# Attention in a fused block: how the softmax's inverse sums reach the output

## The reference, cut to what matters

```python
h = rms_norm(x, attn_norm_g[i])
q, k, v, u, vv = jnp.split(h @ w_in[i], split_at, axis=-1)
q, k = rms_norm and axial_rope of q and k, per head
# gqa_attention, per block of queries:
sc = jnp.einsum('bqkgd,bskd->bkgqs', qblk, k).astype(jnp.float32) * scale
p = jax.nn.softmax(sc, axis=-1).astype(v.dtype)
attn_o = jnp.einsum('bkgqs,bskd->bqkgd', p, v)
sg_o = spatial_gating(gelu(u), gelu(vv), sg_norm_g[i], sg_w[i], sg_b[i])
merged = concat([rms_norm(attn_o, attn_out_g[i]), rms_norm(sg_o, sg_out_g[i])])
x = x + merged @ w_o[i]
# then a gated FFN with a depthwise convolution
```

## Time and profile before

| | |
|---|---|
| median of 3 runs | 2430.03 us (2429.65 to 2431.97) |
| the profiled execution, its own time | 2432.05 us |
| its span in the profile | 2430.2 us |
| TensorE busy | 2377.9 us, 98% of the span |
| VectorE, ScalarE, GpSimd busy | 60%, 44%, 8% |
| chain that ended last | TensorE 84%, VectorE 11%, ScalarE 2% |

### The profile page before, as it was taken

The page is one execution under the profiler, slowest core; times in us unless marked ns, Lnnn a source line. Parts: engine busy times, 40 slices in busy tenths (PEclk is TensorE's granted clock), DMA queues, the critical chain, the costliest instruction groups (busy, mean ns, idle before and its releaser), DMA issues.

```text
span 2430.2 us, 33037 instructions
## 1 busy us (share of the span) xinstructions
PE 2377.9 (98%) x11655; PEld 1939.3 (80%) x11655; DVE 1469.2 (60%) x2142; ACT 1078.0 (44%) x1456; POOL 202.8 (8%) x239
## 2 busy tenths in 40 slices
PE   8999999999999999999999999999999999999999
PEld 6766888888778878888888777888888867888887
DVE  7986654532677646554226867887533686687722
ACT  5345533332555645333225644554423573454421
POOL 2010100000100011000005111000011322000000
PEclk9999999999999999999999999999999999999999
DMA  7331233333222222333334103333334302233331
GB/s 176 70 96 49 82 99 92 101 90 101 71 82 74 78 70 87 95 96 94 94 105 114 56 10 87 104 104 95 93 98 119 101 10 70 87 104 95 91 95 65
DMA packets 403511, 212.30 MB, mean 87 GB/s; under 512 B 19411, under 2 KB 398935, under 8 KB 403431
## 3 DMA queue, kind: packets, MB, share of 16 engines
q1 hardware_dynamic: 397111, 199.65, 28.6%
q0 software_dynamic: 5984, 11.53, 2.0%
q10 hardware_dynamic: 336, 0.05, 0.0%
HBM read 204.38 MB, written 4.19 MB: 86 GB/s over the span
## 4 chain that ended last, share of the span: by engine, by line
PE 84%; DVE 11%; ACT 2%; issue 1%; DVEq 1%; DMA 0%; ACTq 0%; SPq 0%
PE bank L687 69%; PE bank L733 4%; DVE tmp L1958 2%; PE bank L737 2%; DVE w_lo L1926 2%; PE bank L1316 1%; DVEq L1955 1%; DVE small L2711 1%; PE bank L763 1%; PE bank L1290 1%; PE bank L1258 1%; PE bank L1182 0%; PE bank L1128 0%; DVE tmp L1967 0%; PE bank L1219 0%
## 5 line engine op out<-in xcount | busy, mean ns | idle before, releaser
L1926 DVE TENSOR_TENSOR w_lo<-w_raw,w_hi 128x1024 fp32r<-128x1024 f32 x380 | 472.3, 1243 | 522.8 <-ACT w_hi L1390 518.2
L687 PE MATMUL bank<-h_hi,w_hi 128*128 128x512 f32 x1840 | 726.5, 395 | 2.2 <-DVEq L1955 1.2
L687 PE MATMUL bank<-h_lo,w_hi 128*128 128x512 f32 x1840 | 717.9, 390 | 0.0
L687 PE MATMUL bank<-h_hi,w_lo 128*128 128x512 f32 x1840 | 717.6, 390 | 0.0
L1390 ACT ACTIVATE w_hi<-w_raw 128x1024 fp32r<-128x1024 f32 x380 | 401.7, 1058 | 628.1 <-PE bank L687 610.7
L687 PEld LDWEIGHTS bank<-h_hi,w_hi 128*128 128x128 f32 x1840 | 346.6, 188 | 77.5 <-issue 3.8
L687 PEld LDWEIGHTS bank<-h_lo,w_hi 128*128 128x128 f32 x1840 | 346.2, 188 | 72.5
L687 PEld LDWEIGHTS bank<-h_hi,w_lo 128*128 128x128 f32 x1840 | 346.5, 188 | 72.1 <-issue 1.9
L687 PE MATMUL bank<-hid_hi,w_hi 128*128 128x512 f32 x704 | 273.9, 389 | 0.0
L687 PE MATMUL bank<-hid_hi,w_lo 128*128 128x512 f32 x704 | 273.9, 389 | 0.0
L687 PE MATMUL bank<-hid_lo,w_hi 128*128 128x512 f32 x704 | 273.9, 389 | 0.0
(11 more groups left out here) (469 smaller groups left out, 2873.6 us busy)
## 6 DMA issues: line engine op xcount, KB each, us to landing
w_raw<-in_ffn_w SPq DMA_DIRECT2D x120, 512.0 KB, 3.8
w_raw<-in_w_up SPq DMA_DIRECT2D x88, 512.0 KB, 3.8
w_raw<-in_c_w_in SPq DMA_DIRECT2D x32, 512.0 KB, 4.0
w_raw<-in_w_down SPq DMA_DIRECT2D x32, 512.0 KB, 3.6
w_raw<-in_w_in SPq DMA_DIRECT2D x28, 512.0 KB, 3.9
w_raw<-in_w_o SPq DMA_DIRECT2D x16, 512.0 KB, 3.6
w_raw<-in_ab_w_in SPq DMA_DIRECT2D x12, 512.0 KB, 6.1
w_raw<-in_ffn_w SPq DMA_DIRECT2D x16, 384.0 KB, 3.2
```

Source lines behind the costliest of these rows:

```text
L687: mm = nc.tensor.matmul(out[:], w[:, s, k], v[:, kt], start=(kt == 0 and w is w_hi and v is hi), stop=(kt == sum(slabs) - 1 and v is lo))
L1926: nc.vector.tensor_tensor(w_lo[:, s], w_raw[:, s], w_hi[:, s].bitcast(F32), ALU.subtract).then_inc(lo_done, 1)
```

## The change: what it does

Each unit gets its own inverse sum. VectorE takes the reciprocal of one column of `total` per unit (`shares(u)`), GpSimd makes of it a diagonal 128 by 128 (`share_diagonal`: the identity times that column), and T(u) is now four `matmul` calls of `prob` with this diagonal instead of four `transpose` calls with the identity; it waits for `diag_made`. So what is turned is already divided by its sum. The spreads, `keep_share` and `head_out` go. Values are done as whole query tiles: eight products in every second unit from u = 6, instead of four in each. The step from the row maximum to the shift moves from VectorE to GpSimd (`negated_top`, behind a new semaphore `top_ready`). The head outputs are read from the value bank: ScalarE takes the high part and now also the square (`oa_sq`), VectorE the low part, GpSimd only adds the squares. GpSimd's steps are now an order written out by hand as well: in turn u the diagonal of u+1, the shift of u+3, and at u = 5, 7, 9, 11 the squares and sums of a gate tile, at u = 13, 21, 29 the addition for a head pair.

The diff, without the list of semaphore names and unchanged lines:

```diff
@@ -29,7 +29,7 @@
...
 MIX_AT = (4, 6, 8, 10)
-SHARE_AT = (12, 20, 28)
+HEAD_AT = (12, 20, 28)
 SCORE_BANKS = ((2, 3, 4), (0, 1, 4))
@@ -316,11 +316,11 @@
...
         ua_lo = m("ua_lo", [P, 4, SEQ], 8, F32R)
-        oa = m("oa", [P, SEQ], 16)
+        oa_sq = m("oa_sq", [P, SEQ], 16)
+        diag = s5_v[:].rearrange("p v g -> p (v g)").rearrange("p (b q) -> p b q", b=4)
         ua_sum = sq_sum
...
         part_sq = m("part_sq", [P, SEQ], 54)
-        share_all = mixed
         inv_ua = m("inv_ua", [P, SEQ], 48)
...
@@ -582,23 +582,45 @@
...
 
-            def add_parts(ready, parts, total, summed, squared=None):
+            def add_parts(ready, parts, total, summed):
 
...
                     ins = nc.gpsimd.tensor_tensor(square[:], part, part, ALU.mult)
-                    done = squared or pool_part
-                    ins.then_inc(done, 1)
-                    n(done)
+                    ins.then_inc(pool_part, 1)
+                    n(pool_part)
                     if j:
-                        pool.wait_ge(done, n.now(done))
+                        pool.wait_ge(pool_part, n.now(pool_part))
                         last = nc.gpsimd.tensor_tensor(total[:], total[:], part_sq[:], ALU.add)
...
                             pool.wait_ge(pool_part, n(pool_part))
+                    yield
+
+            def share_diagonal(u):
+
+                pool.wait_ge(share_ready, n(share_ready))
+                at_ = u % (4 * TT)
+                nc.gpsimd.tensor_scalar(diag[:, u % 4], ident, share[:, at_:at_ + 1], None, ALU.mult).then_inc(diag_made, 1)
+
+            def add_heads():
+
+                for j in range(4):
+                    pool.wait_ge(oa_squared, n(oa_squared))
+                    if j:
+                        last = nc.gpsimd.tensor_tensor(oa_sum[:], oa_sum[:], oa_sq[:], ALU.add)
+                        last.then_inc(oa_summed if j == 3 else oa_added, 1)
+                    yield
+
+            def negated_top(u):
+
+                c, k = u % 4, 2 * (5 * (u % TT) + u // TT // 2) + u // TT % 2
+                pool.wait_ge(top_ready, n(top_ready))
+                nc.gpsimd.tensor_scalar(shift[:, c:c + 1], top_score[:, c:c + 1], -1.0, head_scale[:, k:k + 1],
+                                        ALU.mult, ALU.mult).then_inc(max_ready, 1)
 
@@ -656,8 +678,21 @@
...
                     n(moved, 16 * 8)
-                add_parts(gated_ready, [ua[:, j] for j in range(4)], ua_sum, ua_summed)
-                add_parts(oa_ready, [oa[:]] * 4, oa_sum, oa_summed, oa_squared)
+                gates = add_parts(gated_ready, [ua[:, j] for j in range(4)], ua_sum, ua_summed)
+                heads = add_heads()
+                for u in range(LOOK):
+                    negated_top(u)
+                share_diagonal(0)
+                for u in range(UNITS):
+                    if u + 1 < UNITS:
+                        share_diagonal(u + 1)
+                    if u + LOOK < UNITS:
+                        negated_top(u + LOOK)
+                    if u - 1 in MIX_AT:
+                        next(gates)
+                    if u - 1 in HEAD_AT:
+                        next(heads)
+                next(heads)
                 add_squares(sq_w)
@@ -1243,21 +1278,20 @@
...
 
-                def values(j, t, keys):
+                def values(j, t):
 
                     b = VALUE_BANKS[i][j % 2]
-                    out = take(b) if (t, keys[0]) == (0, 0) else bank[b]
-                    if (j, t, keys[0]) == (0, 0, 0):
+                    out = bank[b] if t else take(b)
+                    if (j, t) == (0, 0):
                         pe.wait_ge(v_copied, n(v_copied))
-                    if keys[0] == 0:
-                        wait_copies(2 * TT * j + TT + t + 1)
+                    wait_copies(2 * TT * j + TT + t + 1)
                     q = slice(t * P, (t + 1) * P)
-                    for s in keys:
+                    for s in range(TT):
                         for h in (2 * j, 2 * j + 1):
...
                                                   prob_t[h % 4][:, s, q], start=(s == 0), stop=(s == TT - 1))
-                    if (t, s) == (TT - 1, TT - 1):
+                    if t == TT - 1:
                         mm.then_inc(head_done, 1)
@@ -1267,17 +1301,6 @@
...
                     mm.then_inc(v_turned, 1)
-
-                def spread_share(j):
-
-                    out = take(5)
-                    pe.wait_ge(share_ready, n(share_ready))
-                    for t in range(TT):
-                        for hh in range(2):
-                            c = 8 * (j % 2) + TT * hh + t
-                            mm = nc.tensor.matmul(out[HEAD * hh:HEAD * hh + HEAD, t * P:(t + 1) * P],
-                                                  share[:, c:c + 1].to_broadcast([P, HEAD]), ident, start=True, stop=True)
-                    mm.then_inc(share_spread, 1)
 
@@ -1285,9 +1308,10 @@
...
                     out = take(6 + u % 2)
-                    pe.wait_ge(exp_ready, n(exp_ready))
+                    pe.wait_ge(diag_made, n(diag_made))
                     for s in range(TT):
-                        mm = nc.tensor.transpose(out[:, s * P:(s + 1) * P], prob[:, u % 4, s * P:(s + 1) * P], ident)
+                        mm = nc.tensor.matmul(out[:, s * P:(s + 1) * P], prob[:, u % 4, s * P:(s + 1) * P], diag[:, u % 4],
+                                              start=True, stop=True)
                     mm.then_inc(prob_turned, 1)
@@ -1296,15 +1320,12 @@
...
                     if j == 3:
-                        values(3, piece, range(TT))
-                    elif j >= 0:
-                        values(j, piece // 2, range(TT // 2 * (piece % 2), TT // 2 * (piece % 2 + 1)))
+                        values(3, piece)
+                    elif j >= 0 and piece % 2:
+                        values(j, piece // 2)
                     if u in MIX_AT:
                         mix(MIX_AT.index(u))
-                    if u in SHARE_AT:
-                        spread_share(SHARE_AT.index(u))
-                spread_share(3)
-                values(3, TT - 1, range(TT))
+                values(3, TT - 1)
                 merge()
@@ -1807,8 +1828,12 @@
...
 
-                    act.wait_ge(oa_ready, n(oa_ready))
-                    nc.scalar.activation(oa_hi[:, j], oa[:], ACT.Copy, scale=col("attn_gain", 4 * i + j)).then_inc(oa_high, 1)
+                    b = VALUE_BANKS[i][j % 2]
+                    act.wait_ge(head_done, n(head_done))
+                    nc.scalar.activation(oa_hi[:, j], bank[b][:], ACT.Copy, scale=col("attn_gain", 4 * i + j)).then_inc(oa_high, 1)
+                    if j > 1:
+                        act.wait_ge(oa_added, n(oa_added))
+                    nc.scalar.activation(oa_sq[:] if j else oa_sum[:], bank[b][:], ACT.Square).then_inc(oa_squared, 1)
 
@@ -1829,8 +1854,8 @@
...
                         gated_high(MIX_AT.index(u - 3))
-                    if u - 2 in SHARE_AT:
-                        head_high(SHARE_AT.index(u - 2))
+                    if u - 1 in HEAD_AT:
+                        head_high(HEAD_AT.index(u - 1))
                 load_root()
@@ -2708,39 +2733,22 @@
...
                     dve.wait_ge(score_ready, n(score_ready))
-                    step(nc.vector.tensor_reduce(top_score[:, c:c + 1], bank[SCORE_BANKS[i][u % 3]][:], AX.X, ALU.max))
-                    settle()
-                    k = 2 * (5 * (u % TT) + u // TT // 2) + u // TT % 2
-                    own(nc.vector.tensor_scalar(shift[:, c:c + 1], top_score[:, c:c + 1], -1.0, head_scale[:, k:k + 1],
-                                                ALU.mult, ALU.mult), max_ready)
-
-                def shares(j):
-
-                    b = slice(8 * (j % 2), 8 * (j % 2) + 8)
-                    dve.wait_ge(exp_ready, UNITS * i + 2 * TT * (j + 1))
-                    own(nc.vector.reciprocal(share[:, b], total[:, b]), share_ready)
-
-                def keep_share(j):
-
-                    dve.wait_ge(share_spread, n(share_spread))
-                    step(nc.vector.tensor_copy(share_all[:], bank[5][:]))
-                    flag(bank_free[5])
-
-                def head_out(j):
-
-                    dve.wait_ge(head_done, n(head_done))
-                    if j:
-                        dve.wait_ge(oa_squared, n(oa_squared))
-                    settle()
+                    own(nc.vector.tensor_reduce(top_score[:, c:c + 1], bank[SCORE_BANKS[i][u % 3]][:], AX.X, ALU.max), top_ready)
+
+                def shares(u):
+
+                    at_ = u % (4 * TT)
+                    dve.wait_ge(exp_ready, n(exp_ready))
+                    own(nc.vector.reciprocal(share[:, at_:at_ + 1], total[:, at_:at_ + 1]), share_ready)
+
+                def head_low(j):
+
+                    dve.wait_ge(oa_high, n(oa_high))
+                    dve.wait_ge(oa_squared, n(oa_squared))
                     b = VALUE_BANKS[i][j % 2]
```

(61 more changed lines are left out.)

## The result

The changed kernel takes 2473.04 us (median of 4 runs, 2471.46 to 2473.95) against 2429.84 for the one before, a ratio of 1.0172 with a 95% interval of 1.0160 to 1.0184. The forecast was 2463 with a range from 2441 to 2487. The profiled execution has a span of 2471.9 us, 41.7 more than before.

What follows compares the result with a forecast made beforehand. TensorE was taken to bound both attention stages, VectorE not far behind. Work +14.2, waits +14.2 and the clock +5.2 summed to +33.6 us on the median of 2430.03: forecast 2463, range 2441 to 2487.

Steps and rivals of the forecast that it cites:

- the product's price: Attention turns: a plain float32 product is two records, a transpose one, adding 0.45 us to each turn.
- the gates in GpSimd's queue: Units 5, 7, 9, 11: gate squares and sums stand before the diagonal, leaving TensorE idle 9.2 us per stage.
- the start: T(0) waits for last_tile, reciprocal and diagonal: 1.9 us idle; in exchange the 1.10 at T(1) goes.
- the clock: Half speed over T and S behind two of three long gate waits per stage: 5.2 us in all, bounds 0 and 8.
- TensorE is the bound there: Both attention stages: TensorE busy 58.5 of about 64 us bounds them, VectorE at 53 not far behind.
- TensorE's work: Per stage: turns +12.5, values -1.9, spreads -3.5, sum +7.1 us; +14.2 for both.
- GpSimd's prices: GpSimd's new steps: 0.40 us for a diagonal, 0.20 for a shift, bounds 0.10 and 1.29 each.
- today's wait of 1.25: Weight split at u = 16: taken as this wait's cause; it pushes a reciprocal back by 1.2, 0.5 us idle.
- A (queue covered): Rival: gate squares run beside unseen slack, only work counts: +10, 2440 us, or 2446 with little waiting; chance 0.12.
- C (cheap product): Rival: the diagonal product runs at the transpose's 0.44: 2434.8 us, 2430 without the clock's term; chance 0.05.
- D (the factor of four): Rival: the Trainium skill's 4x for FP32 transposes holds, so changed turns cost 56 us more: 2519; chance 0.01.
- B (dear GpSimd steps): Rival: GpSimd's small steps bound each unit; 2475 us from some 0.7 each, 2496 at 1.29; chance 0.14.

Runs made afterwards that it cites:

- the plain turn alone: Kernel before, with each unit's four transposes made plain float32 products with the identity: 2453.45 us, ratio 1.0098.
- split late: Kernel before with whole value tiles, copy before exponential, second exponential before slab, weight split at unit 29, last value tile before last spread: 2424.6 us, ratio 0.9980.

## Why the prediction was right, and where it was short

The time lies in the range, and its parts are the ones that I named: the product's price, the gates in GpSimd's queue, the start, the clock. All three terms of the sum, work, waits and clock, came out larger than forecast over the two loops; no error hid another of size.

- The bound. "TensorE is the bound there" was half right. Added work lands (11.7 of 16 per stage), removed work hardly does (0.3 of 3.6 in the profiled loops, nothing in the times): in the loop before, TensorE takes turns as the bound with ScalarE, and VectorE behind it.
- TensorE's work: forecast +7.1, measured 8.0. Two records per product, read off before the change, decide the case; the plain turn alone is over half of the loss. 0.45 was the price behind scores; behind values it is 0.50. The factor of four that the Trainium skill states for transposes (TensorE: Matmul & The Clock Gate, section Terms) is two in this trace, 0.89 against 0.43.
- The gates' queue: forecast 9.2, measured 9.7 in the first loop and 7.8 in the second, and moving it took 17 us off both stages with the clock behind it. Right, with one thing hidden: VectorE's own gate steps hold the reciprocal back too, 1.8 at T(11).
- GpSimd's prices, a mis-sized term. I took 0.40 for the diagonal and 0.20 for the shift; they took 0.60 and, on the mean, 0.35 (the estimate of 0.19 beside it was further off). Idle after was 15.7 and 14.1, not 12.7, and the excess of the first loop lies mostly in three places: T(18) 1.00 for 0.5, T(23) 1.05 for a part of 0.3, T(31) 1.26 where I had nothing. How much of it is the prices was not run alone. At T(31) it is not the prices: GpSimd's queue held the diagonal behind the addition for a head pair (1.27), which waited for ScalarE's square. That is the queue of the gates once more, in a place that I called covered, and no run moved it.
- One reading was wrong. I took today's wait of 1.25 for the weight split. It is the wait before T(17), and VectorE begins the split at 1409.79, after it; split late shows the same, since the wait is still there. The split does hold back the reciprocal of T(18) in the changed kernel.
- The clock: forecast 2.6 per stage, measured 3.3 and 5.2, and by the wrong waits. (Redone, (1.48 - 0.84) / 3 x 6.6 is 1.4 and not 1.3 each, which adds 0.4 in all.) I tied the fall to the length of the wait. The trace has it behind 1.88 and 3.83 and not behind 2.28 and 2.72 in the first loop, and behind 2.29, 2.42 and 2.26 and not behind 1.88 in the second. The length does not sort them, and that this term came near at all is in part luck.
- Rivals: A (queue covered) and C (cheap product) fell by the rows, D (the factor of four) by the 0.89. B (dear GpSimd steps) can be partly in the result: the diagonal came out at 0.60, between my 0.40 and the 0.7 from which I let B take over.

Both stages together, the forecast was short by 1.8 of work (16.0 for 14.2), 4.4 of waits (29.8 for 25.4) and 3.3 of clock (8.5 for 5.2): 9.5, where 2473 lies 10 above 2463.

## What to carry to other kernels

Replacing a transpose by a product with a scaled identity was free in instructions and not in time here, with float32 data: count the records per call in the profile before, at the same shape. A step given to an idle engine is as late as whatever stands in front of it in that engine's queue, and what waits there for a third engine belongs behind the urgent steps. A longer wait costs more than itself where the clock falls behind it, so read the busy time at an equal number of records as well. Before work is taken off the busiest engine, look at what waits end just before its idle times; here 98% busy did not mean that less work is less time.

## What the runs showed of the hardware that was not expected

A GpSimd instruction of one column took 0.27 alone and 1.15 beside VectorE's subtraction of two 128x1024 tiles, ending with it (first the GpSimd, then the VectorE rows in order of time, changed kernel):

```profile
1425.25 1.15 POOL L622 TENSOR_SCALAR small<-small 128x1 f32<-128x1 f32 x1 [0.82 <-DVE small L2736]
...
1427.04 0.27 POOL L622 TENSOR_SCALAR small<-small 128x1 f32<-128x1 f32 x1
```

```profile
1425.06 1.22 DVE L1951 TENSOR_TENSOR w_lo<-w_raw,w_hi 128x1024 fp32r<-128x1024 f32 x1
```

The Trainium skill (GPSIMD Engine Reference, section 1. Specifications) has GpSimd share its way to SBUF with VectorE, with contention where the latter reads two SBUF inputs; this pair of rows agrees. It lies in the chain of T(18), but ends only 0.05 after the reciprocal for that unit, which stood behind the same subtraction; so most of that wait would be there without it. And an fp32r product of 128 columns takes 0.12 (0.47 for four and their change-over), twice what a quarter of the 0.23 for 512 columns would be.
